# Two weight sums made ahead of the last up block, and the second bank evacuated earlier

## The reference

```python
def squared_relu_mlp(h, w_up, w_down):
    return jnp.square(jax.nn.relu(h @ w_up)) @ w_down      # 1024 -> 4096 -> 1024

for l in range(2):
    ...
    h = modulate(rmsnorm_2(x, norm_g[l, 2]), sh_f, sc_f)
    y = squared_relu_mlp(h, mlp_up_w[l], mlp_down_w[l])
    x = x + g_f[:, None, :] * rmsnorm_2(y, norm_g[l, 3])
```

## Time and profile before

| | before |
|---|---|
| median of three runs | 1758.63 us (1757.03 to 1760.38) |
| the profiled execution | 1758.59 us |
| its span, first to last instruction | 1756.4 us |
| PE busy | 1727.2 us (98%) |
| DVE busy | 1176.9 us (67%) |
| ACT busy | 657.4 us (37%) |
| mean granted clock of PE | 0.995 |

### The profile page before, as it was taken

One profiled execution on the slowest core, in us unless ns is written; L12 is line 12 of the kernel. 1 busy time (PEld: TensorE's weight loads), 2 busy tenths in 40 slices (PEclk: granted clock), 3 DMA queues, 4 the chain that ended last, 5 costly groups with the idle time before them and its releaser, 6 DMA issues. The chain is left out here.

```text
span 1756.4 us, 22656 instructions
## 1 busy us (share of the span) xinstructions
PE 1727.2 (98%) x8568; PEld 1423.8 (81%) x8568; DVE 1176.9 (67%) x1755; ACT 657.4 (37%) x1021; POOL 109.4 (6%) x170
## 2 busy tenths in 40 slices
PE   9999999999999999999999999999999999999998
PEld 8777777888888888888888888887767889797987
DVE  7866555655555667878657575688776886767666
ACT  5236444322222343243414132435344353434341
POOL 0000000000000000101000010002000200000001
PEclk9999999999999999999999999999999999999999
DMA  7321112444454434652255655532312245363641
GB/s 248 109 95 37 49 49 83 154 160 154 143 165 148 142 96 145 216 179 85 86 200 178 206 182 201 172 105 66 104 53 61 72 112 165 86 178 81 171 167 49
DMA packets 64697, 226.20 MB, mean 129 GB/s; under 512 B 7520, under 2 KB 9696, under 8 KB 64416
## 3 DMA queue, kind: packets, MB, share of 16 engines
q1 hardware_dynamic: 45936, 158.10, 27.0%
q0 software_dynamic: 18384, 66.33, 13.8%
q10 hardware_dynamic: 288, 0.59, 0.1%
HBM read 222.11 MB, written 2.10 MB: 128 GB/s over the span
## 5 line engine op out<-in xcount | busy, mean ns | idle before, releaser
L902 ACT ACTIVATE w_hi<-w_raw 128x1024 fp32r<-128x1024 f32 x295 | 310.5, 1053 | 360.8 <-PE psum L2231 240.9
L1321 DVE TENSOR_TENSOR w_lo<-w_raw,w_hi 128x1024 fp32r<-128x1024 f32 x295 | 360.5, 1222 | 116.4 <-ACT w_hi L902 108.8
L2229 PE MATMUL psum<-h_hi,w_hi 128*128 128x512 f32 x1056 | 411.8, 390 | 0.0
L2230 PE MATMUL psum<-h_lo,w_hi 128*128 128x512 f32 x1056 | 410.9, 389 | 0.0
L2231 PE MATMUL psum<-h_hi,w_lo 128*128 128x512 f32 x1056 | 410.8, 389 | 0.0
L2229 PEld LDWEIGHTS psum<-h_hi,w_hi 128*128 128x128 f32 x1056 | 198.2, 188 | 41.9 <-issue 0.5
L2230 PEld LDWEIGHTS psum<-h_lo,w_hi 128*128 128x128 f32 x1056 | 198.3, 188 | 41.4 <-issue 0.5
L2231 PEld LDWEIGHTS psum<-h_hi,w_lo 128*128 128x128 f32 x1056 | 198.2, 188 | 41.1
L2229 PE MATMUL psum<-hid_hi,w_hi 128*128 128x512 f32 x536 | 208.5, 389 | 0.0
L2230 PE MATMUL psum<-hid_lo,w_hi 128*128 128x512 f32 x536 | 208.5, 389 | 0.0
L2231 PE MATMUL psum<-hid_hi,w_lo 128*128 128x512 f32 x536 | 208.5, 389 | 0.0
(11 more groups left out here) (377 smaller groups left out, 2580.1 us busy)
## 6 DMA issues: line engine op xcount, KB each, us to landing
w_raw<-in_wstream SPq DMA_DIRECT2D x283, 512.0 KB, 4.1
ada_raw<-in_ada POOLq DMA_DIRECT2D x112, 512.0 KB, 3.9
w_diff<-in_wstream SPq DMA_DIRECT2D x6, 512.0 KB, 6.4
w_raw<-in_wstream POOLq DMA_DIRECT2D x6, 512.0 KB, 5.6
w_diff<-in_wstream POOLq DMA_DIRECT2D x6, 512.0 KB, 5.5
x<-in_xT SPq DMA_DIRECT2D x8, 256.0 KB, 5.3
outT<-x SPq DMA_DIRECT2D x16, 128.0 KB, 1.8
con<-in_consts SPq DMA_DIRECT2D x1, 1032.0 KB, 9.9
```

Of the source, the lines that this page charges most:

```text
L902: act.activation(w_hi[:, slot, :], w_raw[:, slot, :], ACT.Copy).then_inc(whi_done, 1)
L1321: dve.tensor_tensor(w_lo[:, slot, :], w_raw[:, slot, :], w_hi[:, slot, :].bitcast(F32), ALU.subtract).then_inc(wlo_done, 1)
L2229: pe.matmul(bank, w_hi[:, slot, w], hi[:, ra + k, :], start=k == 0, stop=False)
L2230: pe.matmul(bank, w_hi[:, slot, w], lo[:, ra + k, :], start=False, stop=False)
```

## The change

The first two weight sums of each stage (those of B and C in its first quad) leave the stage's step t = 0 and are made by DVE in the step of the last up block, behind its split and ahead of its product; the sums of the second quad stay where they were. In the step t = 1 of a stage DVE evacuates its product (A11) ahead of the split (that of C) instead of behind it. `weight_sum` and the evacuation, now `evacuate`, are the same instructions as before.

```diff
             def quads(s):
                 n0, o0 = s["at"]["n"], s["at"]["o"]
...
-                sums = [n0 + Q * QUAD + u for Q in range(QUADS) for u in (U_B, U_C)]
+                sums = [n0 + Q * QUAD + u for Q in range(1, QUADS) for u in (U_B, U_C)]
                 for t in range(QUADS * QUAD):
                     Q, u = divmod(t, QUAD)
                     n, o = n0 + t, o0 + t
                     while sums and sums[0] <= n + AHEAD + 1:
                         weight_sum(sums.pop(0))
                     m = n + AHEAD
+                    if t == 1:
+                        evacuate(Q, u, o)
                     if SOURCE[m][0] == U_D:
...
                     else:
                         split_lo(m, m % SPLIT)
+                    if t != 1:
+                        evacuate(Q, u, o)
...
                     elif evac == "relu2" and s.get("paired"):
                         i, odd = divmod(t.b, 2)
+                        if t.b == s["nblk"] - 1:
+                            for u in (U_B, U_C):
+                                weight_sum(at_["n"] + s["nblk"] + u)
                         dve.wait_ge(gate_done, at_["gate"] + t.b + 1)
```

More of the change, by code:

```diff
@@ L1427, in pair_sums, with weight_sum @@
                 dve.scalar_tensor_tensor(out=g4, in0=g2, scalar=-1.0, in1=b21, op0=ALU.mult, op1=ALU.subtract).then_inc(pair_step, 1)
+            def weight_sum(n):
+                u, _, quad = SOURCE[n]
+                slot, before = n % RAW, (n - 1) % RAW
+                other = (n - 2) % RAW if u == U_B else slot
+                for m in (n - 1, n - 2 if u == U_B else n - 4):
+                    dve.wait_ge(raw_loaded[m % RAW], 16 * (m // RAW + 1))
+                dve.wait_ge(wlo_done, n - RAW + 1)
+                dve.tensor_tensor(w_raw[:, slot, :], w_raw[:, before, :], w_raw[:, other, :], ALU.add)\
+                   .then_inc(raw_loaded[slot], 16)
+                dve.wait_ge(raw_loaded[slot], 16 * (n // RAW + 1))
+                dve.sem_inc(sum_made, 1)
@@ L1429, in quads @@
             def quads(s):
                 n0, o0 = s["at"]["n"], s["at"]["o"]
[L1432 to L1443, removed]
@@ L1445, in of_tiles, with evacuate @@
                 def of_tiles(Q, i, h):
                     return y[:, 4 * Q + i:4 * Q + i + 3:2, half_of(h)]
-                sums = [n0 + Q * QUAD + u for Q in range(QUADS) for u in (U_B, U_C)]
[L1450 to L1462, removed]
+                def evacuate(Q, u, o):
@@ L1479, in quads @@
                     z.then_inc(bank_free, 1)
+                sums = [n0 + Q * QUAD + u for Q in range(1, QUADS) for u in (U_B, U_C)]
+                for t in range(QUADS * QUAD):
+                    Q, u = divmod(t, QUAD)
+                    n, o = n0 + t, o0 + t
+                    while sums and sums[0] <= n + AHEAD + 1:
+                        weight_sum(sums.pop(0))
+                    m = n + AHEAD
+                    if t == 1:
+                        evacuate(Q, u, o)
+                    if SOURCE[m][0] == U_D:
+                        dve.wait_ge(whi_done, m + 1)
+                        dve.tensor_tensor(w_lo[:, m % SPLIT, :], w_diff[:, :], w_hi[:, m % SPLIT, :].bitcast(F32),
+                                          ALU.subtract).then_inc(wlo_done, 1)
+                        dve.sem_inc(raw_loaded[m % RAW], 16)
+                    else:
+                        split_lo(m, m % SPLIT)
+                    if t != 1:
+                        evacuate(Q, u, o)
             def gemm(s, last):
```

## The result

| | before | after |
|---|---|---|
| median, four runs of each on one chip | 1758.97 us (1757.03 to 1760.38) | 1745.66 us (1745.04 to 1746.19) |
| the profiled execution | 1758.59 us | 1746.19 us |
| its span | 1756.4 us | 1743.9 us |
| mean granted clock of PE | 0.995 | 0.997 |

The ratio is 0.9925 (95% interval 0.9908 to 0.9942): 13.3 us faster. The forecast was 1747.6 us, with a range of 1743.0 to 1753.1. The time is right; on the path to it two terms were wrong, and the three stages went three different ways.

The account below looks back on a forecast made before the run. TensorE, busy 1727.2 of 1756.4 us, bounds the kernel, with three waits on DVE's evacuation. Stage gains of 3.80, 3.44 and 3.80 us, capped by the second quad's chain, sum to 11.04: 1758.59 to 1747.6 us, range 1743.0 to 1753.1.

Parts of the forecast that it names:

- The hole: DVE's idle 3.27 us ahead of the last up block's product; the two sums, 2.91 to 3.24 us, fit at no cost.
- The second cover: If the hole closes, PE starts A 0.32 us after the last up block's low parts end, hiding that much lateness.
- The first quad's wait and its clock: PE's wait of about 3.58 us ahead of B and 2.41, 1.55 and 1.57 us of lower clock go, in three stages.
- The full gain: PE gains 5.99, 5.14 and 5.15 us by the start of C in the three stages, 16.28 us in all.
- The chain of the second quad: A's loads, then DVE's work up to A11's evacuation, 8.03 us behind the landing, cap the gain at B; chain moves 3.05 us.
- D's split moves by 3.25 us: B's split starts near 1438.1 instead of 1441.36, so D's split and SyncE's load behind it come 3.25 us earlier.
- Two loads 0.6 us closer cost 0.2 us: C's split gains 0.6 us less, so two 512 KB loads come closer; cost between 0 and 0.6 us, taken as 0.2.
- The landing of 7.1 us: First stage's slow accumulating load in the second quad, place or chance: 0 or 1.5 us more gain, taken as 0.75.
- the rival, given a chance of 0.18: Clock falls again behind the second quad's new waits: 1750.0 us if in the first stage alone, 1753.1 in all three; chance 0.18.
- the rival that gains everything: The second quad's chain shortens as well, so no wait replaces the old one: all 16.28 us, 1742.3 us; chance 0.12.
- the case that was given 0.62: The forecast itself: the wait moves into the second quad ahead of B, mostly shorter, at 2.2, 1.7 and 1.35 us.
- the spare of the forecast: Time the second quad's chain had to spare before B: 0, 0.39 and 0.75 us in the three stages.

Follow-up runs that it names:

- the two extra sums: Changed kernel with two more unused 128x1024 sums by DVE ahead of the last up block's product: 1750.96 us, ratio 0.9955 to before.
- the sums alone: Changed kernel with A11 evacuated behind C's split again, so only the two sums moved: 1749.26 us, and 1746.37 us in a second series.
- the evacuation alone: Changed kernel with the two sums back at t = 0, so only A11's evacuation moved: 1756.65 us, ratio 0.9984 to before.
- A's load first: Changed kernel with SyncE's load of the second quad's A issued right behind the first quad's A22: 1741.82 us, ratio 0.9902 to before.
- the second execution: The changed kernel itself, unaltered, run and traced again beside the kernel with only the sums moved: 1745.18 us.

## Why the prediction was right, and where it was not

- **The hole took the two sums at no cost: right.** It had 0.59 us left in every stage, the product behind came no later against the stage's start, and the two extra sums show what an overfull hole looks like. The second cover was read at the wrong place: PE is held up first at the fourth pair's products, not at A, and the cover there is 0.45 us, not 0.32.
- **The first quad's wait and its clock are gone: right**, 3.58 us and the clock in all three stages. The two edits are both needed for it: with the sums alone 0.55 us stay, with the evacuation alone 2.64 us. The full gain was put too low, though, at 16.28 us: with A's load first, which has no wait left in a stage, the three stages are 17.12 us shorter than before. Counted from start to start each wait had cost 3.74 us, and in the first stage the lower clock had reached into C as well (3.13 us instead of 2.88).
- **The chain of the second quad is next: right.** The releaser is the one named, A11's evacuation, and from the landing to its end it is 8.03 us as forecast (1455.53 to 1462.88 + 0.68). Three waits of about 5 us together were expected behind it; there are two, of 2.6 us, because the chain moved by more. DVE and the queues in the changed kernel's first stage:

```profile
1443.30 0.33 SPq L815 DMA_DIRECT2D w_raw<-in_wstream  x1
...
1449.73 0.86 POOL L857 DMA_DIRECT2D w_raw<-in_wstream  x1 [21.87 <-DMA w_raw<-in_wstream]
```

```profile
1455.53 1.23 DVE L1437 TENSOR_TENSOR w_raw<-w_raw 128x1024 f32<-128x1024 f32 x1 [4.02 <-issue]
...
1462.88 0.68 DVE L1466 TENSOR_TENSOR y<-y,psum 128x512 f32<-128x512 f32 x1
```

- **D's split moves by 3.25 us: 0.42 too much.** It moved by 2.83 us in each stage. B's split could not follow the low parts at once: it waits 0.21 us for ScalarE's copy, and A11's evacuation starts 0.11 us behind A12's end. Before the change neither was there.
- **Two loads 0.6 us closer cost 0.2 us: the wrong sign.** This step failed. From SP's load of A to the accumulating load it took 6.44, 6.39 and 6.02 us before and 6.43, 5.46 and 4.36 us after: 0.01, 0.93 and 1.66 us less. By the means over all executions the closer load is worth 6.32 - 5.55 = 0.77 us. The bound "between 0 and 0.6 us" left out a gain without a row that excluded one.
- **The landing of 7.1 us was chance, not place.** In the rows before it is 1459.76 - 1452.52 = 7.24 us; after, 1455.53 - 1449.73 = 5.80 us, and no later execution had more than 5.88 us in that place (one load in another stage took 6.28). The forecast took half of it, 0.75 us; the first stage got 1.44.
- **The clock: the rival, given a chance of 0.18, happened in one stage of three.** The chain moved by more than forecast in the first stage, but the wait of 2.00 us left there cost 1.56 us of clock, which the likeliest sum did not hold: 2.79 us gained instead of 3.80. The forecast had put a rival on it and priced it at 2.41 us. Its reason against, that the new waits would be only 1.35 to 2.2 us, did not hold: the one of 2.00 us was enough, though the second execution waited 1.56 us in the same place and kept its clock.

By stage the forecast was 3.80, 3.44 and 3.80 us, and 2.79, 4.48 and 5.31 came: in the first the clock fell again, in the second the wait moved as forecast, but was shorter, and the third is the rival that gains everything. So the case that was given 0.62 is what one stage shows, and the others show two of its rivals. By the parts above the chain moved by 2.83 + 0.01 + 1.44 = 4.28, 2.83 + 0.93 + 0.39 = 4.15 and 2.83 + 1.66 + 0.25 = 4.74 us (split, load of A, landing). With the spare of the forecast (0, 0.39 and 0.75) and less 1.56 for the clock that is 2.72, 4.54 and 5.49, within 0.1 us of what came, but for the third stage, which has reached its floor at 5.31. So the sum of 11.04 was 1.5 us short, and the time is right partly because errors of both signs met. The Trainium skill (TensorE: Matmul & The Clock Gate, HAM oscillation) says that a kernel whose TensorE idles long enough at a time falls back to the lower clock and pays for it anew each time. The runs agree for the waits of 3.58 us; behind those of 2.0 to 2.65 us the clock fell in some cases and not in others, and behind shorter ones it did not fall.

What the change left behind, 3.8 us by the medians (2.5 and 4.5 us by the stages of the two executions), is had by issuing the second quad's A earlier (1741.82 us). That the whole of it lay in one load's place in SP's list shows that the chain, and no other limit, stood in the way.

## What to carry to other kernels

When work moves into an engine's hole, follow the next chain that ends on the same tile: here it was a DMA that waits for a split made by the moved engine, and its term decided the gain. Ahead of pricing a load's new place, look whether it can be issued earlier altogether, since a load at the front of its queue made the question of its landing time disappear. A wait of about 2 us or more on TensorE is priced with its clock as a range: here it cost its own length, or about one and a half to two and a half microseconds more.

## What the runs showed of the hardware

- **The same wait does not always lower the clock.** The granted clock behind a wait of PE in the stages: 3.58 or 3.59 us, lower in three of three; 2.64 or 2.65 us, lower in two of three (0.61, 0.50, then 1.00); 2.40 us lower (0.64); 2.15 us not; 2.00 us lower (0.62); 1.73, 1.71, 1.56, 1.42 us and all shorter ones not. Between 2.0 and 2.65 us the length of the wait alone does not tell, and what does was not found.
- **A load of 512 KB issued closer behind another was ready sooner,** on average 6.32, 5.55 and 5.19 us at distances of 1.7, 1.1 and 0.4 us (12, 18 and 3 loads, which scatter by 1 us and more); the forecast had it the other way.
- **The place of a kernel's start in time scatters.** The first stage began 1.75 us later in one execution of the changed kernel than in the other (1434.50 and 1432.75 us), so stages are compared by their own lengths.
